# The recurrent gates of a two-layer hybrid trunk: from split operands to plain fp32 in 64x64 tiles

## The chip, the cores and the metric
One core of one Trainium2 chip. The time is the device time of one execution of the whole program in microseconds; lower is better. Three runs of the kernel before gave 2337.05, 2337.07 and 2337.18 us; the median, 2337.07, is the time before.

## The reference
Two layers over 1024 positions of 2048 features in fp32. Each layer makes six parts from one projection of the normalized input, runs two mixers on them, gates both, and projects back. The change concerns `r` and `i` of the second mixer alone: 16 diagonal blocks of 64x64 weights each, applied to the convolved input.

```
h = rmsnorm(x, norm_gain[l])
q, k, v, g_attn, x_rnn, g_rnn = split(h @ w_in[l])
attn = swa_sink_attention(q, k, v, sinks)        # window of two chunks of 64
xc = causal_conv(x_rnn, conv_w, conv_b)          # width 4
xb = xc.reshape(b, s, 16, 64)
r = sigmoid(einsum('bshi,hij->bshj', xb, w_r) + b_r)
i = sigmoid(einsum('bshi,hij->bshj', xb, w_i) + b_i)
log_a = -8 * r * softplus(-lru_param)
u = sqrt(-expm1(2 * log_a)) * (i * xc)
rnn = associative_scan(a = exp(log_a), u)
x = x + concat(attn * silu(g_attn), rnn * silu(g_rnn)) @ w_out[l]
```

After the second layer a last rmsnorm closes the trunk.

## The kernel before
**Tiling.** Features lie on the 128 partitions, positions in the free dimension. The sequence is worked in two halves of 512 positions (`h`), each through both layers (`l`). The projections are the bulk: per layer 25 groups (17 in, 8 out) of two 128-feature tiles over 16 tiles of input. They run as units. A unit is one slot `s` of 200 per layer; it takes a 128x512 piece of weights (two input tiles by 256 output features) and issues 12 matmuls of 128x512 (line 420).

**Splitting.** These matmuls have fp32r operands. To keep fp32 accuracy each operand is split in two parts: ScalarE copies it to fp32r (the high part), VectorE subtracts that from the original (the low part), and three products are added up: high by high, high by low, low by high. For weights that is `weight_hi` (line 636) and `weight_lo` (line 995), four buffers in a ring, three units ahead of TensorE.

**Order.** Each engine has a hand-written loop over `h`, `l`, `s`; at given slots other work is put behind or ahead of the unit. On TensorE these are scores (line 504), transposes of the probabilities (line 522) and values (line 534) at slots 36, 44, ... (`VISIT`), and the recurrent gates at `R0[j] + 5` and `R0[j] + 7`. `R0` is the slot at which the projection of recurrent tile `j` is complete: 48, 56, 64, 72, 88, 96, 104, 112.

**A recurrent tile** holds two blocks of 64 features, so its gates need four products with 64x64 weights: two blocks times `r` and `i`. After the projection VectorE scales (`conv`, slot `R0`), then makes the four taps of the convolution into `xc` (`taps`, slots `R0 + 1` and `R0 + 2`). ScalarE copies the gate weights to fp32r (`gate_weights_hi`, line 785) and the two blocks of `xc` (`conv_hi`, line 793), VectorE subtracts (`gate_weights_lo`, line 1169, and `conv_lo`, line 1176). The two parts of one block lie above each other in `xcut`, 64 partitions the high part and 64 the low part, and the weights of that block stand twice below each other in `gw`. So one matmul over 128 rows gives weight part times both parts of the input, two matmuls (one per part of the weights) give one block's `r` and `i`. This is `gate(h, l, j, part)`, line 553, once for each block:

```
for a in range(2):
    last = pe.matmul(ps_g[:, :], gwcut[:, part, a, :], xcut[:, part, :], start=a == 0, stop=a == 1)
```

Both blocks write the same PSUM bank `ps_g`, the second once ScalarE has read the first (`gate_out`, lines 803 and 805, slots `R0 + 6` and `R0 + 8`: two tanh of 64x512 each). The recurrence follows on both engines in slots `R0 + 9` to `R0 + 13`. `ps_g` and its neighbour `ps_t` also take the transposes.

**Queues.** All large loads are issued by SyncE in the order of the slots: the projection weights (line 335), each waiting for the low part of the unit in hand, and at slot `R0[j] - 8` the gate weights of tile `j` (line 359) into one of two buffers.

**Plain fp32 calls.** Scores, values and transposes take fp32 operands unsplit. Scores are 16 calls per visit with 64 rows, 64 columns of weights and 128 of data, in all four quarters of the array (two row halves, two column halves), the row halves into two banks. Values are 4 calls with 128 rows, 64 columns of weights and 256 of data, in the two column halves.

Of the kernel before, what the change touches and what calls it, by code (L numbers as in the profile page):

```python
# [7 lines left out]
F32 = mybir.dt.float32  # L8
# [5 lines left out]
P = 128  # L14
# [5 lines left out]
HD = 64  # L20
# [87 lines left out]
def build(nc, xt, w, gates, par, fgain, cossin, ident, out):  # L108
    with ExitStack() as ctx:
# [26 lines left out]
        acc = sb("acc", [TOK])  # L136
        gw = sb("gw", [GRING, 2, P])
        gwcut = sb("gwcut", [2, 2, P], F32R)
        khist = sb("khist", [DEPTH, CH])
# [26 lines left out]
        ps_tok = ps_t[:, 0, 0:HT // P]  # L166
        ps_half = ps_g[:, 0:HT]
        ps_ss = ps_t[:, :, :].rearrange("p a b -> p (a b)")

# [21 lines left out]
        op_hi = sem("op_hi")  # L191
        gw_hi = sem("gw_hi")
        xc_hi = sem("xc_hi")
        sq_done = sem("sq_done")
# [18 lines left out]
        op_lo = sem("op_lo")  # L213
        gw_lo = sem("gw_lo")
        xc_lo = sem("xc_lo")
        acc_done = sem("acc_done")
# [94 lines left out]
        def _(sp_):  # L311
# [16 lines left out]
            for h in range(HALVES):  # L328
                for l in range(DEPTH):
                    for s in range(SLOTS):  # L330
                        u = h * UNITS + l * SLOTS + s

                        sp_.wait_ge(w_lo, u + 1)
                        ahead = (u + RING if u + RING < TOTAL else u + RING - UPG) % UNITS
                        sp_.dma_start(wraw[:, u % RING, :],
                                      w[ahead // SLOTS, ahead % SLOTS]).then_inc(w_in[u % RING], 16)
                        if u + 3 < KT // 2:
                            x_load(0, u + 3)
                        if l == 0 and s in (4, TAB_LD):

                            sp_.wait_ge(q_done, per_layer(h, s // TAB_LD, AT, 1))
                            sp_.dma_start(tab[:, 0, :], cossin[0, h]).then_inc(tab_in, 16)
                            sp_.dma_start(tab[:, 1, :], cossin[1, h]).then_inc(tab_in, 16)
                        if l == 0 and s == 60:

                            if h > 0:
                                sp_.wait_ge(out_done_s, 16 * len(STORES_W) * h)
                            sp_.dma_start(x[:, :, :], xt[h]).then_inc(xres_in, 16)
                        for a, b in STORES_W:
                            if h > 0 and l == 0 and s == NS + 2 * b:  # L350

                                sp_.wait_ge(scaled, (h - 1) * KT + b)
                                sp_.dma_start(out[h - 1, :, a:b, :], x[:, a:b, :]).then_inc(out_done_s, 16)
                        if s + 8 in R0:
                            j = R0.index(s + 8)
                            n = l * RT + j

                            sp_.wait_ge(gw_lo, h * (DEPTH * RT) + (n + 1))
                            sp_.dma_start(gw[:, n % GRING, :, :], gates[l, j]).then_inc(gw_in[n % GRING], 16)
                        if l == 1 and s == O0 + 12 and h < LAST:  # L360

                            sp_.wait_ge(op_lo, at_op(h, 1, 1, KT - 1))
                            for i in range(KT // 2):
                                x_load(h + 1, i)
# [24 lines left out]
        def _(pe):  # L389
# [4 lines left out]
            pe.sem_inc(vt_done, 1)  # L394
            pe.sem_inc(g_done, 2 * GRING)

# [112 lines left out]
            def prob_transposes(h, l, p):  # L509
# [4 lines left out]
                else:  # L514
                    pe.wait_ge(vtok_done, per_layer(h, l, 2, 2))
                gates_read = sum(r + 7 < VISIT[p + 1] for r in R0)
                if gates_read:
# [19 lines left out]

            def gate(h, l, j, part):

                n = l * RT + j  # L540
                if part == 0:

                    pe.wait_ge(xc_lo, per_layer(h, l, 2 * RT, 2 * j + 2))
                    pe.wait_ge(gw_lo, h * (DEPTH * RT) + (n + 1 + GRING))
                    copied = sum(v < R0[j] + 5 for v in VISIT[1:NP + 1])
                    pe.wait_ge(pt_done, per_layer(h, l, NB, 2 * copied))
                    if j > 0:
                        pe.wait_ge(i_done, per_layer(h, l, 2 * RT, 2 * j))
                else:

                    pe.wait_ge(i_done, per_layer(h, l, 2 * RT, 2 * j + 1))
                for a in range(2):
                    last = pe.matmul(ps_g[:, :], gwcut[:, part, a, :], xcut[:, part, :], start=a == 0, stop=a == 1)  # L553
                last.then_inc(g_done, 1)

            for h in range(HALVES):
                for l in range(DEPTH):
                    for s in range(SLOTS):
# [20 lines left out]
                        for j in range(RT):  # L579
                            if s in (R0[j] + 5, R0[j] + 7):  # L580
                                gate(h, l, j, (s - R0[j] - 5) // 2)
            for i in range(UPG - 2):
# [43 lines left out]
        def _(act):  # L626
# [152 lines left out]

            def gate_weights_hi(h, l, j):  # L780
                n = l * RT + j

                act.wait_ge(gw_in[n % GRING], h * (16 * DEPTH * RT // GRING) + (16 * (n // GRING) + 16))
                act.wait_ge(g_done, h * (2 * DEPTH * RT) + (2 * n + 2 * GRING))
                act.activation(gwcut[:, :, 0, :], gw[:, n % GRING, :, :], ACT.Copy).then_inc(gw_hi, 1)

            def conv_hi(h, l, j):

                act.wait_ge(conv_done, per_layer(h, l, RT, j + 1))
                act.wait_ge(g_done, per_layer(h, l, 2 * RT, 2 * j) + 2 * GRING)  # L790
                for part in range(2):
                    rows = slice(HD * part, HD * part + HD)
                    act.activation(xcut[rows, part, :], xc[rows, :], ACT.Copy).then_inc(xc_hi, 1)  # L793

            def gate_out(h, l, j, part):

                act.wait_ge(g_done, per_layer(h, l, 2 * RT, 2 * j + part + 1) + 2 * GRING)
                if j > 0 and part == 0:
                    act.wait_ge(m2_done, per_layer(h, l, RT, j))
                if j > 1 and part == 0:  # L800
                    act.wait_ge(scan_done, per_layer(h, l, RT, j - 1))
                a, b = HD * part, HD * (1 - part)
                act.activation(r_in[a:a + HD, :], ps_g[a:a + HD, :], ACT.Tanh, scale=0.5,  # L803
                               bias=pars[a:a + HD, l, C_BR + j:C_BR + j + 1]).then_inc(r_done, 1)
                act.activation(i_in[j % 2][a:a + HD, :], ps_g[b:b + HD, :], ACT.Tanh, scale=0.5,
                               bias=pars[b:b + HD, l, C_BI + j:C_BI + j + 1]).then_inc(i_done, 1)
# [42 lines left out]
            for h in range(HALVES):  # L849
                for l in range(DEPTH):  # L850
                    for s in range(SLOTS):
# [58 lines left out]
                        if s == VT_TR + 1:  # L910
                            for i in range(2):
                                v_copy(h, l, i)
                        if s - 3 in R0:
                            conv_hi(h, l, R0.index(s - 3))
                        if s - 1 in G0:
# [5 lines left out]
                        for j in range(RT):  # L921
                            if s == R0[j] + 2:
                                gate_weights_hi(h, l, j)
                            if s == R0[j] + 10:
# [49 lines left out]
        def _(dve):  # L974
            dve.sem_inc(evac, 4)
            dve.sem_inc(q_done, 1)
            dve.sem_inc(gw_lo, GRING)
            dve.memset(eps[:, :], EPS).then_inc(dve_set, 1)
# [174 lines left out]

            def taps(h, l, j, part):
                for c in (0, 1) if part == 0 else range(2, CW):
                    wc = pars[:, l, C_CW + CW * j + c:C_CW + CW * j + c + 1]
# [6 lines left out]
                    else:  # L1163
                        dve.scalar_tensor_tensor(xc[:, :], src, wc, xc[:, :], ALU.mult, ALU.add).then_inc(conv_done, 1)

            def gate_weights_lo(h, l, j):
                n = l * RT + j
                dve.wait_ge(gw_hi, h * (DEPTH * RT) + (n + 1))
                dve.tensor_tensor(gwcut[:, :, 1, :], gw[:, n % GRING, :, :], gwcut[:, :, 0, :].bitcast(F32),
                                  ALU.subtract).then_inc(gw_lo, 1)  # L1170

            def conv_lo(h, l, j):
                for part in range(2):
                    a, b = HD * part, HD * (1 - part)
                    dve.wait_ge(xc_hi, per_layer(h, l, 2 * RT, 2 * j + part + 1))
                    dve.tensor_tensor(xcut[b:b + HD, part, :], xc[a:a + HD, :],  # L1176
                                      xcut[a:a + HD, part, :].bitcast(F32), ALU.subtract).then_inc(xc_lo, 1)

# [64 lines left out]
            for h in range(HALVES):  # L1243
                for l in range(DEPTH):
                    for s in range(SLOTS):
# [20 lines left out]
                        if s - 2 in R0:  # L1266
                            taps(h, l, R0.index(s - 2), 1)
                        if s - 4 in R0:
                            conv_lo(h, l, R0.index(s - 4))
                        if s - 3 in R0:  # L1270
                            gate_weights_lo(h, l, R0.index(s - 3))
                        for k in range(X_EARLY if h else RING, KT):
# [175 lines left out]
```

## Time and profile before

| | before |
|---|---|
| median of the runs, us | 2337.07 |
| span of the profiled execution, us | 2335.3 |
| TensorE busy, us | 2328.8 |
| VectorE busy, us | 1389.5 |
| ScalarE busy, us | 1257.0 |
| projection matmuls (line 420), busy us | 2176.9 |
| recurrent gate matmuls (line 553), busy us | 39.8 |
| copies of the convolution to its high part (line 793), busy us | 40.4 |
| subtractions for its low part (line 1176), busy us | 43.9 |

The page gives the profiled execution by its span, from the first to the last instruction; the device time of a run, about 1.8 us more, holds what lies around it. Busy times of one engine overlap for matmuls, which are pipelined: a matmul of 128x512 is on record for about 390 ns, and the next begins before it ends. The price of a group of matmuls is therefore read from starts, not from durations.

### The profile page before, as it was taken

To read this page: it belongs to the slowest core of one execution; us is meant where nothing else is said; L and a number is where in the kernel's file an instruction comes from. 1 tells how busy PE (TensorE), PEld (TensorE's weight loads), DVE (VectorE), ACT (ScalarE), POOL (GpSimd) and SP (SyncE) were. 2 spreads that over 40 slices of the span, in tenths; PEclk is the share of its full clock that TensorE was granted. 3 is DMA by queue.
4 is the path that set the end of the run, shared out by engine and by line. 5 is a ranking of instruction groups with operands and counts; after the bars stand their busy time and mean duration, and the time that the engine had idled before them with its cause. 6 is when DMAs were issued, how large, how long until landed. Compare 5 with 4: busy or idle time off the path is not lost.

```text
span 2335.3 us, 31126 instructions
## 1 busy us (share of the span) xinstructions
PE 2328.8 (100%) x11466; PEld 1916.2 (82%) x11466; DVE 1389.5 (60%) x2239; ACT 1257.0 (54%) x2379; POOL 0.8 (0%) x10
## 2 busy tenths in 40 slices
PE   9999999999999999999999999999999999999999
PEld 8888888888888888888888888888888888888888
DVE  7557667434546767744475676764354467676335
ACT  7457666324445767534464576652244557665333
POOL 0000000000000000000000000000000000000000
PEclk9999999999999999999999999999999999999999
DMA  5334323333332233353334432233333332323334
GB/s 192 102 108 144 93 89 94 100 95 100 95 98 86 84 93 88 95 171 92 99 113 137 171 108 88 88 100 95 98 96 95 93 93 84 89 91 96 99 95 140
DMA packets 127016, 244.42 MB, mean 105 GB/s; under 512 B 14352, under 2 KB 18704, under 8 KB 126096
## 3 DMA queue, kind: packets, MB, share of 16 engines
q1 hardware_dynamic: 126288, 242.28, 33.7%
q8 instruction: 90, 1.47, 0.3%
q14 instruction: 62, 0.51, 0.1%
q10 hardware_dynamic: 576, 0.16, 0.0%
HBM read 234.00 MB, written 8.39 MB: 104 GB/s over the span
## 4 chain that ended last, share of the span: by engine, by line
PE 100%; DVE 0%; issue 0%; POOL 0%; POOLq 0%
PE proj L420 93%; PE ps_sc L504 1%; PE proj L534 1%; PE ps_g L553 1%; PE proj L436 1%; PE ps_g L522 1%; PE ps_t L522 1%; PE proj L463 0%; PE ps_t L392 0%; PE ps_t L478 0%; PE proj L612 0%; PE ps_t L488 0%; PE ps_g L488 0%; PE ps_sc L612 0%; PE ps_t L592 0%; DVE mixed L1388 0%
## 5 line engine op out<-in xcount | busy, mean ns | idle before, releaser
L420 PE MATMUL proj<-operand,wcut 128*128 128x512 f32 x9480 | 2176.9, 390 | 0.0
L420 PEld LDWEIGHTS proj<-operand,wcut 128*128 128x128 f32 x9480 | 1776.7, 188 | 378.6 <-issue 7.0
L995 DVE TENSOR_TENSOR wcut<-wraw,wcut 128x512 fp32r<-128x512 f32 x804 | 555.0, 690 | 878.2 <-ACT wcut L636 874.8
L636 ACT ACTIVATE wcut<-wraw 128x512 fp32r<-128x512 f32 x803 | 506.3, 631 | 900.0 <-PE proj L420 882.6
L761 ACT ACTIVATE prob<-ps_sc,stat 128x128 f32<-128x128 f32 x256 | 89.7, 362 | 0.6
L719 ACT ACTIVATE gy<-proj 32x512 f32<-32x512 f32 x144 | 84.9, 589 | 3.8
L793 ACT ACTIVATE xcut<-xc 64x512 fp32r<-64x512 f32 x64 | 40.4, 631 | 44.6 <-issue 23.0
L676 ACT ACTIVATE sqr<-x 128x512 f32<-128x512 f32 x62 | 36.8, 635 | 45.9 <-DVE x L1207 45.7
L1024 DVE TENSOR_TENSOR acc<-acc,sqr 128x512 f32<-128x512 f32 x80 | 55.2, 691 | 4.9
L761 ACT ACTIVATION_READ_ACCUMULATOR prob<-ps_sc,stat 128x1 f32 x256 | 51.6, 202 | 0.0
L1162 DVE SCALAR_TENSOR_TENSOR xc<-xr,pars,xc 128x512 f32<-128x512 f32 x64 | 47.9, 749 | 1.4
L1006 DVE TENSOR_TENSOR operand<-mixed,operand 128x512 fp32r<-128x512 f32 x64 | 41.7, 688 | 10.3 <-ACT operand L658 9.6
L824 ACT ACT_TABLE_LOAD x32 | 41.1, 1283 | 11.7 <-DVE mu L1192 11.3
L1176 DVE TENSOR_TENSOR xcut<-xc,xcut 64x512 fp32r<-64x512 f32 x64 | 43.9, 686 | 2.1
L803 ACT ACTIVATE sqr<-ps_g,pars 64x512 f32<-64x512 f32 x64 | 43.7, 683 | 1.3
L1207 DVE TENSOR_TENSOR x<-proj,x 128x512 f32<-128x512 f32 x62 | 39.9, 685 | 2.2 <-PE proj L420 1.3
L749 ACT ACTIVATE gt<-gy 128x512 f32<-128x512 f32 x56 | 35.5, 633 | 8.3 <-DVE gy L1108 7.0
L1120 DVE TENSOR_TENSOR mixed<-mixed,gy 128x512 f32<-128x512 f32 x56 | 38.8, 692 | 1.9
L1144 DVE TENSOR_TENSOR prob<-prob,stat 128x1024 f32<-128x1024 f32 x32 | 39.2, 1225 | 1.1
L1130 DVE TENSOR_REDUCE stat<-ps_sc 128x8 f32<-128x1024 f32 x32 | 39.2, 1224 | 1.1
L553 PE MATMUL ps_g<-xcut,gwcut 128*128 128x512 f32 x128 | 39.8, 391 | 0.0
L1103 DVE TENSOR_TENSOR gy<-proj,rstd 128x512 f32<-128x512 f32 x56 | 38.6, 689 | 1.4
(161 smaller groups left out, 1200.4 us busy)
## 6 DMA issues: line engine op xcount, KB each, us to landing
wraw<-in_w SPq DMA_DIRECT2D x804, 256.0 KB, 2.6
x<-in_xt SPq DMA_DIRECT2D x2, 4096.0 KB, 12.8
mixed<-in_xt SPq DMA_DIRECT2D x14, 512.0 KB, 7.3
gw<-in_gates SPq DMA_DIRECT2D x32, 128.0 KB, 2.6
out<-x SPq DMA_DIRECT2D x4, 1024.0 KB, 4.9
out<-mixed SPq DMA_DIRECT2D x7, 512.0 KB, 2.6
tab<-in_cossin SPq DMA_DIRECT2D x8, 256.0 KB, 3.4
mixed<-in_xt SPq DMA_DIRECT2D x4, 256.0 KB, 3.7
```

The source lines that it names most:

```text
L420: last = pe.matmul(bank[:, :], wcut[:, u % RING, a, c:c + P], operand[:, k, b, :], start=(k == 0 and n == 0), stop=(k == KT - 1 and n == 2))
L522: last = pe.transpose(ps_tr[i][:, 2 * odd + pair, :], prob[:, odd, i, pair, :], idn[:, :])
L553: last = pe.matmul(ps_g[:, :], gwcut[:, part, a, :], xcut[:, part, :], start=a == 0, stop=a == 1)
L636: act.activation(wcut[:, u % RING, 0, :], wraw[:, u % RING, :], ACT.Copy).then_inc(w_hi, 1)
L719: act.activation(gy[dst:dst + 32, 1, :], bank_of(l, tile)[src:src + 32, :], ACT.Copy).then_inc(shift_done, 1)
L761: act.activation(prob[:, odd, i, pair, :], ps_s[:, odd, i, pair, :], ACT.Exp, scale=HD ** -0.5, bias=stat[:, 1, odd, i, pair:pair + 1], ac ...
L803: act.activation(r_in[a:a + HD, :], ps_g[a:a + HD, :], ACT.Tanh, scale=0.5, bias=pars[a:a + HD, l, C_BR + j:C_BR + j + 1]).then_inc(r_done, 1)
L995: dve.tensor_tensor(wcut[:, u % RING, 1, :], wraw[:, u % RING, :], wcut[:, u % RING, 0, :].bitcast(F32), ALU.subtract).then_inc(w_lo, 1)
L1006: dve.tensor_tensor(operand[:, k, 1, :], mixed[:, k, :], operand[:, k, 0, :].bitcast(F32), ALU.subtract).then_inc(op_lo, 1)
L1024: ins = dve.tensor_tensor(acc[:, :], acc[:, :], sqr[:, k % 2, :], ALU.add)
L1162: mark(dve.scalar_tensor_tensor(xc[:, :], src, wc, xc[:, :], ALU.mult, ALU.add))
L1176: dve.tensor_tensor(xcut[b:b + HD, part, :], xc[a:a + HD, :], xcut[a:a + HD, part, :].bitcast(F32), ALU.subtract).then_inc(xc_lo, 1)
```

## The change
The gates are no longer split. `gw` holds the fp32 weights once: its upper 64 rows are block 0, `[w_r | w_i]`, its lower 64 rows block 1, `[w_i | w_r]`. `gate(h, l, j)` is one visit at slot `R0[j] + 5` and issues four fp32 calls of 64 rows, 64 columns of weights and 512 of data, one per block and gate: block 0 into bank `ps_t`, block 1 into `ps_g`, the two gates of a block into the two halves of the partitions. The first block's tanhs read `ps_t`, the second's `ps_g`, at the slots of before. The four split steps on ScalarE and VectorE go, with their semaphores. The gate load on SyncE is half as large and waits for TensorE's visit two tiles earlier; the first tap of a tile waits for the visit of the tile before, which reads `xc`.

```diff
-        gw = sb("gw", [GRING, 2, P])
-        gwcut = sb("gwcut", [2, 2, P], F32R)
+        gw = sb("gw", [GRING, P])
...
+        ps_gate = [ps_t[:, :, :].rearrange("p a b -> p (a b)"), ps_g]
...
-                            sp_.wait_ge(gw_lo, h * (DEPTH * RT) + (n + 1))
-                            sp_.dma_start(gw[:, n % GRING, :, :], gates[l, j]).then_inc(gw_in[n % GRING], 16)
+                            sp_.wait_ge(g_done, h * (DEPTH * RT) + (n + 1))
+                            sp_.dma_start(gw[:, n % GRING, :], gates[l, j]).then_inc(gw_in[n % GRING], 16)
...
-            pe.sem_inc(g_done, 2 * GRING)
+            pe.sem_inc(g_done, GRING)
...
-                gates_read = sum(r + 7 < VISIT[p + 1] for r in R0)
+                gates_read = sum(r + 5 < VISIT[p + 1] for r in R0)
...
-            def gate(h, l, j, part):
+            def gate(h, l, j):
 
                 n = l * RT + j
-                if part == 0:
-
-                    pe.wait_ge(xc_lo, per_layer(h, l, 2 * RT, 2 * j + 2))
-                    pe.wait_ge(gw_lo, h * (DEPTH * RT) + (n + 1 + GRING))
-                    copied = sum(v < R0[j] + 5 for v in VISIT[1:NP + 1])
-                    pe.wait_ge(pt_done, per_layer(h, l, NB, 2 * copied))
-                    if j > 0:
-                        pe.wait_ge(i_done, per_layer(h, l, 2 * RT, 2 * j))
-                else:
-
-                    pe.wait_ge(i_done, per_layer(h, l, 2 * RT, 2 * j + 1))
-                for a in range(2):
-                    last = pe.matmul(ps_g[:, :], gwcut[:, part, a, :], xcut[:, part, :], start=a == 0, stop=a == 1)
+                pe.wait_ge(conv_done, per_layer(h, l, RT, j + 1))
+                pe.wait_ge(gw_in[n % GRING], h * (16 * DEPTH * RT // GRING) + (16 * (n // GRING) + 16))
+                copied = sum(v < R0[j] + 5 for v in VISIT[1:NP + 1])
+                pe.wait_ge(pt_done, per_layer(h, l, NB, 2 * copied))
+                if j > 0:
+                    pe.wait_ge(i_done, per_layer(h, l, 2 * RT, 2 * j))
+                for col in range(2):
+                    for blk in range(2):
+                        rows = slice(HD * blk, HD * blk + HD)
+                        last = pe.matmul(ps_gate[blk][HD * col:HD * col + HD, :], gw[rows, n % GRING, HD * col:HD * col + HD],
+                                         xc[rows, :], start=True, stop=True)
                 last.then_inc(g_done, 1)
...
-            def gate_weights_hi(h, l, j):
...
-            def conv_hi(h, l, j):
...
-                act.activation(r_in[a:a + HD, :], ps_g[a:a + HD, :], ACT.Tanh, scale=0.5,
+                act.activation(r_in[a:a + HD, :], ps_gate[part][a:a + HD, :], ACT.Tanh, scale=0.5,
...
-                act.activation(i_in[j % 2][a:a + HD, :], ps_g[b:b + HD, :], ACT.Tanh, scale=0.5,
+                act.activation(i_in[j % 2][a:a + HD, :], ps_gate[part][b:b + HD, :], ACT.Tanh, scale=0.5,
...
             def taps(h, l, j, part):
+                if part == 0:
+                    dve.wait_ge(g_done, per_layer(h, l, RT, j) + GRING)
...
-            def gate_weights_lo(h, l, j):
...
-            def conv_lo(h, l, j):
...
-    gates = np.tile(np.stack([first, second], axis=3), (1, 1, 2, 1, 1))
+    gates = np.concatenate([first, second], axis=2)
```

How TensorE's list runs from one pass of scores to the next transposes, before (`proj` is a bank of the projections, `ps_sc` the scores, `ps_t` and `ps_g` the two shared banks; line 420 is the projection, line 553 the gates, line 522 the transposes):

```order
L504 MATMUL ps_sc<-kboth,q 64x128 x16
L420 MATMUL proj<-operand,wcut 128x512 x12
L553 MATMUL ps_g<-xcut,gwcut 128x512 x2
L420 MATMUL proj<-operand,wcut 128x512 x24
L553 MATMUL ps_g<-xcut,gwcut 128x512 x2
L420 MATMUL proj<-operand,wcut 128x512 x60
L522 MATMUL ps_t<-idn,prob 128x128 x4
```

The same place with the change (lines 500, 416, 546 and 518 are scores, projection, gates and transposes there):

```order
L500 MATMUL ps_sc<-kboth,q 64x128 x16
L416 MATMUL proj<-operand,wcut 128x512 x12
L546 MATMUL ps_t<-xc,gw 64x512
L546 MATMUL ps_g<-xc,gw 64x512
L546 MATMUL ps_t<-xc,gw 64x512
L546 MATMUL ps_g<-xc,gw 64x512
L416 MATMUL proj<-operand,wcut 128x512 x84
L518 MATMUL ps_t<-idn,prob 128x128 x4
```

The second visit is gone, and the 24 and 60 projections around it are one run of 84; the first visit holds four calls in two banks.

SyncE's queue around the gate weights' loads in the first layer, before (`w_lo` is the split of a unit's weights, `gw_lo` that of the gate weights):

```order
L335 DMA wraw<-in_w 128x512 [waits w_lo] x2
L359 DMA gw<-in_gates 128x256 [waits gw_lo]
L335 DMA wraw<-in_w 128x512 [waits w_lo] x8
L359 DMA gw<-in_gates 128x256 [waits gw_lo]
L335 DMA wraw<-in_w 128x512 [waits w_lo] x4
```

And with the change (`g_done` counts the visits on TensorE):

```order
L331 DMA wraw<-in_w 128x512 [waits w_lo] x2
L355 DMA gw<-in_gates 128x128 [waits g_done]
L331 DMA wraw<-in_w 128x512 [waits w_lo] x8
L355 DMA gw<-in_gates 128x128 [waits g_done]
L331 DMA wraw<-in_w 128x512 [waits w_lo] x4
```

The places are the same; size and semaphore differ.

## Rows read from the trace of the kernel before

**Rows 1.** The page's head: span, busy time by engine, chain that ended last.
```profile
span 2335.3 us, 31126 instructions
...
PE 2328.8 (100%) x11466; PEld 1916.2 (82%) x11466; DVE 1389.5 (60%) x2239; ACT 1257.0 (54%) x2379; POOL 0.8 (0%) x10
...
PE 100%; DVE 0%; issue 0%; POOL 0%; POOLq 0%
```

**Rows 2.** Waits: waiting engine and line, what it waited for, us, times, longest.
```profile
ACT wcut L636 <- PE proj L420: 882.6, 515, 3.4
```

**Rows 3.** Chain that ended last, two pieces: start us, us, what, count.
```profile
11.11 29.93 PE proj L420 x132
...
2105.64 195.88 PE proj L420 x864
```

**Rows 4.** Windows around these pieces: length, busy by engine, clock (last but two).
```profile
10.90:40.00 29.10, 29.10 (x130) 24.09 (x130) 27.25 (x42) 25.81 (x43) 0.00 (x0) 1.00 0.65 229
2106.00:2300.00 194.00, 194.00 (x857) 160.72 (x856) 90.27 (x136) 77.60 (x125) 0.00 (x0) 1.00 0.33 97
```

**Rows 5.** TensorE's groups by form: count, busy us, mean ns, idle before.
```profile
L553 PE MATMUL ps_g<-xcut,gwcut 128*128 128x512 f32 x128 | 39.8, 391 | 0.0
L504 PE MATMUL ps_sc<-kboth,q 64*64 64x128 f32 x1024 | 35.3, 276 | 0.0
L534 PE MATMUL proj<-probT,vtok 128*64 128x256 f32 x256 | 34.7, 392 | 0.0
```

**Rows 6.** Timeline of TensorE, scores to transposes with gates: start us, us, what.
```profile
157.51 3.03 PE L420 MATMUL proj<-operand,wcut 128*128 128x512 f32 x12
160.38 0.62 PE L553 MATMUL ps_g<-xcut,gwcut 128*128 128x512 f32 x2
160.84 5.65 PE L420 MATMUL proj<-operand,wcut 128*128 128x512 f32 x24
...
180.43 0.60 PE L522 MATMUL ps_t<-idn,prob 128*128 128x128 f32 x4
```

**Rows 7.** The same, scores to transposes without gates.
```profile
107.64 1.10 PE L504 MATMUL ps_sc<-kboth,q 64*64 64x128 f32 x32
108.67 22.10 PE L420 MATMUL proj<-operand,wcut 128*128 128x512 f32 x96
130.61 0.60 PE L522 MATMUL ps_t<-idn,prob 128*128 128x128 f32 x4
```

**Rows 8.** The same, values between two pairs of gates, then no values.
```profile
320.29 13.80 PE L420 MATMUL proj<-operand,wcut 128*128 128x512 f32 x60
334.02 1.08 PE L534 MATMUL proj<-probT,vtok 128*64 128x256 f32 x8
335.04 3.06 PE L420 MATMUL proj<-operand,wcut 128*128 128x512 f32 x12
337.94 0.62 PE L553 MATMUL ps_g<-xcut,gwcut 128*128 128x512 f32 x2
...
344.34 16.53 PE L420 MATMUL proj<-operand,wcut 128*128 128x512 f32 x72
360.71 0.62 PE L553 MATMUL ps_g<-xcut,gwcut 128*128 128x512 f32 x2
```

**Rows 9.** Narrow windows in scores and values: start of the first, time until the last ends.
```profile
107.64 0.34 PE L504 MATMUL ps_sc<-kboth,q 64*64 64x128 f32 x4
107.64 0.45 PE L504 MATMUL ps_sc<-kboth,q 64*64 64x128 f32 x8
...
334.02 0.44 PE L534 MATMUL proj<-probT,vtok 128*64 128x256 f32 x2
334.02 0.65 PE L534 MATMUL proj<-probT,vtok 128*64 128x256 f32 x4
```

**Rows 10.** Timeline of SyncE's queue, one gate load and the next projection load.
```profile
156.53 0.43 SPq L359 DMA_DIRECT2D gw<-in_gates  x1
162.09 0.33 SPq L335 DMA_DIRECT2D wraw<-in_w  x1
```

More of the change, by code:

```diff
@@ L191, in build @@
         op_hi = sem("op_hi")
-        gw_hi = sem("gw_hi")
-        xc_hi = sem("xc_hi")
         sq_done = sem("sq_done")
@@ L213, in build @@
         op_lo = sem("op_lo")
-        gw_lo = sem("gw_lo")
-        xc_lo = sem("xc_lo")
         acc_done = sem("acc_done")
@@ L579, in _ @@
                         for j in range(RT):
-                            if s in (R0[j] + 5, R0[j] + 7):
-                                gate(h, l, j, (s - R0[j] - 5) // 2)
+                            if s == R0[j] + 5:
+                                gate(h, l, j)
             for i in range(UPG - 2):
@@ L778, in attn_out @@
                 act.activation(to, value_bank(l, p), ACT.Copy).then_inc(attn_done, 1)
-            def gate_weights_hi(h, l, j):
[L781 to L785, printed above, removed]
-            def conv_hi(h, l, j):
[L789 to L793, printed above, removed]
             def gate_out(h, l, j, part):
-                act.wait_ge(g_done, per_layer(h, l, 2 * RT, 2 * j + part + 1) + 2 * GRING)
+                act.wait_ge(g_done, per_layer(h, l, RT, j + 1) + GRING)
                 if j > 0 and part == 0:
@@ L912, in _ @@
                                 v_copy(h, l, i)
-                        if s - 3 in R0:
-                            conv_hi(h, l, R0.index(s - 3))
                         if s - 1 in G0:
@@ L921, in _ @@
                         for j in range(RT):
-                            if s == R0[j] + 2:
-                                gate_weights_hi(h, l, j)
                             if s == R0[j] + 10:
@@ L976, in _ @@
             dve.sem_inc(q_done, 1)
-            dve.sem_inc(gw_lo, GRING)
             dve.memset(eps[:, :], EPS).then_inc(dve_set, 1)
@@ L1164, in taps @@
                         dve.scalar_tensor_tensor(xc[:, :], src, wc, xc[:, :], ALU.mult, ALU.add).then_inc(conv_done, 1)
-            def gate_weights_lo(h, l, j):
[L1167 to L1170, printed above, removed]
-            def conv_lo(h, l, j):
[L1173 to L1177, printed above, removed]
             def lru_z(h, l, j):
@@ L1267, in _ @@
                             taps(h, l, R0.index(s - 2), 1)
[L1268 to L1271, printed above, removed]
                         for k in range(X_EARLY if h else RING, KT):
```

## The prediction
> **What bounds the kernel now.** I read the page's head first: TensorE is busy for 2328.8 of 2335.3 us, and the chain that ended last is TensorE to 100% [rows 1]. Then the waits: ScalarE stood 882.6 us in 515 waits of its weight splitting, each of them for TensorE to free a buffer [rows 2]. So the time is the sum of what TensorE issues, and an instruction taken off ScalarE or VectorE is worth nothing by itself. The profiled execution has a span of 2335.3 us; the median of the runs is 2337.07, 1.8 us more for what lies around the span. I make the sum against the span and add the 1.8 back. About 0.2% (4.7 us) is what a measurement of this kernel can tell from no change.
>
> **The unit of account.** Every price below is a detour: what the projection stream loses when something else stands in it. The stream runs at one matmul in 0.2267 us: 195.88 us for 864, 29.93 us for 132 [rows 3], with the granted clock at 1.00, the 2.4 GHz level [rows 4].
>
> **What the change removes on TensorE.** Two visits per tile, 32 tiles (2 halves, 2 layers, 8), each of two 128x512 matmuls; the profile has the 128 of them [rows 5]. Between a pass of scores and the next transposes stand 96 projections. Where the gates of one tile lie among them, they take 180.43 - 157.51 = 22.92 us [rows 6]; where none do, 130.61 - 108.67 = 21.94 [rows 7]. The gates of a tile thus cost 0.98 us. A second way: a pair takes 160.84 - 160.38 = 0.46 from its start to the next projection [rows 6], and the 72 projections between two pairs take 360.71 - 344.34 = 16.37 [rows 8], 0.05 more than 72 x 0.2267 = 16.32. Twice 0.51 is 1.02. I take 1.01 (the second way is free of what scores leave behind), or 32.3 us in all.
>
> **What it adds on TensorE.** One visit per tile: four fp32 calls of 64x64 with 512 columns, on four distinct quarters of the array. No row of before shows this form. The two nearest are scores (16 fp32 calls in 64x64, 128 columns, all four quarters) and values (4 fp32 calls of 128x64, 256 columns, two column halves). Three things are to be seen in them.
> First, an fp32 call becomes two MATMUL records: 1024 for 32 visits x 16 calls, 256 for 32 x 4 [rows 5].
> Second, calls on different quarters run side by side, in steps. Of scores, the first four records are over after 0.34 us and the first eight after 0.45: a step of 0.11 for four records. Of values it is two records at a time, over after 0.44 and 0.65: a step of 0.21 to 0.22 [rows 9]. The step doubles with the columns (128 to 256) and does not grow with the number of quarters that share it; with 512 columns I extend it to 0.43.
> Third, all three then have the same length of steps: scores 32/4 = 8 of 0.11, values 8/2 = 4 of 0.215, the new gates 8/4 = 2 of 0.43, each 0.86 to 0.87.
> What is left is entering and leaving another tiling. One visit of values stands alone in the stream, between two gate pairs: 72 projections and the values take 337.94 - 320.29 = 17.65 us, against 16.37 for 72 projections between the same neighbours [rows 8]. It costs 1.28 us, so 0.42 above its steps. From its start to the next projection a visit of values takes 335.04 - 334.02 = 1.02 [rows 8], one of scores 108.67 - 107.64 = 1.03 [rows 7], so four quarters enter and leave about as two halves do.
> The gates have two steps where values have four. Since 2 x 0.11 exceeds 0.215 by 0.005, a step saved is worth next to nothing; I take 1.27. Bounds: above, 1.31, the 1.28 of values, the 0.01 that scores take more, and 0.02 for four differences of rows rounded to 0.01. Below, 1.21: the 1.02 of values hold four steps of 0.215 and 0.16 of start and end; how this divides the rows don't tell, and I let a smaller share of it, 0.06, vanish under a step of 0.43.
>
> **The sum.** 32 x (1.27 - 1.01) = +8.3 us; with 1.21 - 1.02 it is +6.1, with 1.31 - 0.98 it is +10.6. Span 2335.3 + 8.3 = 2343.6, time 2337.1 + 8.3 = **2345.4 us**.
>
> **What it takes off the others, priced at nothing.** ScalarE loses, per tile, two 64x512 copies and the copy of the gate weights, VectorE the three subtractions that go with them. The cover is TensorE's own stream, for which both wait [rows 2]. The four tanh evacuations of a tile stay in their slots.
>
> **What moves or waits.** (a) The visit stays where part 0 was, 12 projections after scores, so it shares no entry with them; the visit 24 later is gone. (b) TensorE waits for the convolution itself, not for its split: by the lists VectorE ends it three units (of 12 projections) ahead, the split was one unit ahead. (c) The gates now also write the bank of the transposes; the next transposes come 84 projections (19 us) later, and the tanhs that free it stand within three units (8 us). (d) VectorE's first tap of the next tile waits for the visit of this one; behind it stand the weight splits, but the tap comes four units after the visit. (e) On SyncE's queue the gate weights' load waited for a split that was long done; it now waits for TensorE's visit two tiles earlier. Where these lie 16 units apart (half of them) this bites: the load went at 156.53 [rows 10], and the visit it would wait for starts at 160.38 [rows 6] and ends near 161.6. Behind it stands the next projection load, which went at 162.09 anyway [rows 10]; the gate load takes 0.43, so the other is late by 0.1 us at most, and the ring holds four units of weights (10.9 us). Price 0. If that cover were gone, each half-microsecond late would be paid 16 times, 8 us.
>
> **Rivals.**
> *The column halves run in series* (slower still). Then the visit has four steps, not two: 0.86 us more, and 32 x 0.86 + 8.3 = +35.8, 2372.9 us. It decides if a quarter cannot take its weights while its neighbour in the same rows streams. For it: here the issue goes over the row halves first, in scores over the column halves. Against it: in scores two pairs share their rows, and still four records are over together [rows 9]. The Trainium skill, "TensorE: Matmul & The Clock Gate", Packing small matmuls, says that a weight load overlaps with running matmuls only if its row group differs. By that rule this rival would be the forecast; the scores rows speak against it.
> *Entering and leaving cost nothing* (not slower). Then a visit is 0.86, and 32 x (0.86 - 1.01) = -4.8: 2332.3 us, at the edge of what can be told. It decides if weights and data that are ready long before let the array change its tiling while the last projection drains; with 0.15 of the 0.42 left it is no change. Against it: the operands of values are ready units before their turn too, and the 0.42 are paid [rows 8]. The same section of the Trainium skill models a packed group as one matmul and 4 ns per further tile, with no price for the ends; by it this rival would be the forecast, and the trace disagrees with it by the 0.42.
> *The relief of the other engines shortens the stream* (faster). 9480 projections would have to gain 0.9 ns each to cancel 8.3 us and 1.4 ns to come out 4.7 us ahead, at 2332.4. Against it: with VectorE busy 27.25 and ScalarE 25.81 of 29.10 us [rows 4] the step is 29.93/132 = 0.2267; with 90.27 and 77.60 of 194.00 it is 195.88/864 = 0.2267 [rows 3].
>
> **How the numbers follow.** Forecast 0.88, its own range 2343.2 to 2347.7 (+6.1 to +10.6). Columns in series 0.06, ends free or nearly so 0.04, relief 0.02. Slower by over 0.2%: 0.88 + 0.06 = 0.94. Within 0.2%: 0.04 of the second rival, less 0.01 for its edge, 0.03. Faster: 0.02 + 0.01 = 0.03. With 0.88 inside its bounds the forecast alone holds the 8 in 10, and the range is its own.
>
> **What would show it.** Gate MATMUL records: 256 instead of 128, in two groups of four per visit, the second about 0.43 after the first. From the visit's start to the next projection about 1.0 us. The 96 projections with a gate visit take about 23.2 us, not 22.92. TensorE busy for the whole span, the stream's step still 0.2267, ScalarE and VectorE less busy without effect. It is wrong if there are four groups (then near 2373), if the visit takes under 0.9 us (then the ends are cheaper), or if the projections begin to wait for split weights (then SyncE's new wait counts).

## The result, and the profile after

The changed kernel takes 2346.05 us, median of four runs (2345.93 to 2346.47); the kernel before, four runs beside them, 2337.12 (2337.05 to 2337.38). The ratio is 1.0039, with a 95% interval of 1.0024 to 1.0053: slower by 8.9 us. The forecast was 2345.4, with a range of 2343.2 to 2347.7.

| | before | after |
|---|---|---|
| median, us | 2337.12 | 2346.05 |
| span of the profiled execution, us | 2335.3 | 2344.2 |
| VectorE busy, us | 1389.5 | 1336.3 |
| ScalarE busy, us | 1257.0 | 1205.4 |
| gate records on TensorE | 128 | 256 |

The page's head of the changed kernel, as [rows 1]:

```profile
span 2344.2 us, 31157 instructions
...
PE 2337.3 (100%) x11594; PEld 1895.8 (81%) x11594; DVE 1336.3 (57%) x2143; ACT 1205.4 (51%) x2283; POOL 0.8 (0%) x10
```

TensorE still fills the span. VectorE and ScalarE have 53 and 52 us less to do, and the time went up. Its timeline from one pass of scores to the next transposes, as [rows 6]:

```profile
157.79 3.02 PE L416 MATMUL proj<-operand,wcut 128*128 128x512 f32 x12
160.74 0.64 PE L546 MATMUL ps_t<-xc,gw 64*64 64x512 f32 x1
160.74 0.64 PE L546 MATMUL ps_g<-xc,gw 64*64 64x512 f32 x1
160.75 0.64 PE L546 MATMUL ps_t<-xc,gw 64*64 64x512 f32 x1
160.75 0.64 PE L546 MATMUL ps_g<-xc,gw 64*64 64x512 f32 x1
161.22 0.59 PE L546 MATMUL ps_t<-xc,gw 64*64 64x512 f32 x1
...
161.75 19.36 PE L416 MATMUL proj<-operand,wcut 128*128 128x512 f32 x84
180.95 0.60 PE L518 MATMUL ps_t<-idn,prob 128*128 128x128 f32 x4
```

Four records start within 0.01 us, the next four 0.48 later, and the stream goes on 161.75 - 160.74 = 1.01 after the start. The 96 projections with a gate visit take 180.95 - 157.79 = 23.16 us, against 22.92 in [rows 6]. The same price without scores beside it, as [rows 8]:

```profile
340.06 0.64 PE L546 MATMUL ps_t<-xc,gw 64*64 64x512 f32 x1
...
341.08 22.07 PE L416 MATMUL proj<-operand,wcut 128*128 128x512 f32 x96
363.08 0.64 PE L546 MATMUL ps_t<-xc,gw 64*64 64x512 f32 x1
```

96 projections between two visits take 22.00, which is 0.24 more than 96 x 0.2267 = 21.76. With 1.02 for the visit itself the detour costs 1.26 us. The same reading of the kernel before gave 2 x 0.51 = 1.02. So both readings, 23.16 against 22.92 and 1.26 against 1.02, put 0.24 us more on each tile.

One place was not in the sum: the sixth tile of a layer, whose visit follows the last transposes.

```profile
310.63 0.60 PE L518 MATMUL ps_t<-idn,prob 128*128 128x128 f32 x4
...
312.61 3.03 PE L416 MATMUL proj<-operand,wcut 128*128 128x512 f32 x12
313.23 0.64 ACT L803 ACTIVATE mu<-mu 128x512 f32<-128x512 f32 x1
...
314.91 0.59 ACT L764 ACTIVATE probT<-ps_g 128x512 f32<-128x512 f32 x1
...
315.73 0.13 PEld L546 LDWEIGHTS ps_t<-xc,gw 64*64 64x64 f32 x1 [0.51 <-issue]
315.76 0.61 PE L546 MATMUL ps_t<-xc,gw 64*64 64x512 f32 x1
```

Here 12 projections and the entry take 315.76 - 312.61 = 3.15 us instead of 160.74 - 157.79 = 2.95. ScalarE ended its copy out of `ps_g` at 315.50, and the gate's first weight load came 0.23 later. This happens once in each of the four layer passes. In the kernel before the same copy was in time:

```profile
309.05 0.60 PE L522 MATMUL ps_t<-idn,prob 128*128 128x128 f32 x4
...
312.83 0.59 ACT L770 ACTIVATE probT<-ps_g 128x512 f32<-128x512 f32 x1
...
313.88 0.62 PE L553 MATMUL ps_g<-xcut,gwcut 128*128 128x512 f32 x2
```

It ended at 313.42, 4.37 after the transposes began and 0.46 before the gates. Now it ends 315.50 - 310.63 = 4.87 after them.

One more piece of the difference between the two profiled executions is older than the first gate. In the chain that ended last, the piece that began at 11.11 and took 29.93 us [rows 3] reads now:

```profile
11.19 30.12 PE proj L416 x132
```

It ends at 41.31 instead of 41.04, 0.27 us late, before any line of the change has run; in the profiles of the experiments below the first matmul of this line starts anywhere from 10.8 to 11.6 us (10.9 before, 11.1 here), and none of them changes what comes ahead of it.

### The profile page after: what moved, and what is told of

Its sections match the earlier page's. It is cut to its first block, busy times and chain, and to the rows that moved or that the text cites. A ratio compares the mean times of both kernels' runs of the same rounds, so it can differ in the third digit from the quotient of the medians.

```text
span 2344.2 us, 31157 instructions
## 1 busy us (share of the span) xinstructions
PE 2337.3 (100%) x11594; PEld 1895.8 (81%) x11594; DVE 1336.3 (57%) x2143; ACT 1205.4 (51%) x2283; POOL 0.8 (0%) x10
## 4 chain that ended last, share of the span: by engine, by line
PE 100%; DMA 0%; DVE 0%; issue 0%; SPq 0%; DVEq 0%
PE proj L416 92%; PE ps_sc L500 1%; PE proj L530 1%; PE ps_t L546 1%; PE proj L432 1%; PE ps_t L518 1%; PE ps_g L518 1%; PE proj L459 0%; DMA wraw<-in_w 0%; PE ps_t L474 0%; PE ps_g L484 0%; PE proj L606 0%; PE ps_t L484 0%; PE ps_sc L606 0%; PE ps_t L586 0%; PE ps_g L546 0%
## 5 line engine op out<-in xcount | busy, mean ns | idle before, releaser
L1082 DVE SCALAR_TENSOR_TENSOR gy<-gt,gy 128x512 f32<-128x512 f32 x56 | 38.5, 687 | 1.0
L652 ACT ACTIVATE operand<-mixed 128x512 fp32r<-128x512 f32 x64 | 37.2, 622 | 0.8
L500 PEld LDWEIGHTS ps_sc<-kboth,q 64*64 64x64 f32 x1024 | 27.6, 133 | 11.3 <-issue 11.3
L500 PE MATMUL ps_sc<-kboth,q 64*64 64x128 f32 x1024 | 35.3, 276 | 0.0
```

Of the source, the lines that this page charges most:

```text
L500: last = pe.matmul(ps_s[HD * m:HD * m + HD, odd, i, pair, :], q[rows, TPK * kv + 2 * pair + m, CH * c:CH * c + CH], kboth[rows, kv, CH * c ...
```

## Experiments

There are eight kernels, the first four on one chip and the last four on another, each time with runs of the kernel before between them: 2337.00 us beside the first four, 2336.95 beside the last four.

**Are the ends a fixed price per visit, or does each group of calls pay them?**

```diff
-                for col in range(2):
+                for col in (0, 1, 0, 1):
                     for blk in range(2):
```

> The four calls of each gate visit are issued twice in a row (the second time over the same results). Theory: a visit is a fixed price for entering and leaving the 64x64 tiling, 0.42 us, and 0.43 us for each step of four records side by side. Then two steps more add 0.86 us per visit, 32 x 0.86 = 27.5 us: 2346.1 + 27.5 = 2373.6 us, and the trace shows a visit start to next projection of 1.88 us instead of 1.02. Rival: the 0.42 us belong to each group of four calls (a drain per group): 32 x 1.27 = 40.6 us more, 2386.7. Rival: calls that return to a quarter in use run in series, over 2400.

Measured: 2372.75 us, 26.7 above the changed kernel. Timeline of TensorE in one visit:

```profile
160.69 0.64 PE L546 MATMUL ps_t<-xc,gw 64*64 64x512 f32 x1
...
161.17 0.59 PE L546 MATMUL ps_t<-xc,gw 64*64 64x512 f32 x1
...
161.60 0.59 PE L546 MATMUL ps_t<-xc,gw 64*64 64x512 f32 x1
...
162.03 0.59 PE L546 MATMUL ps_t<-xc,gw 64*64 64x512 f32 x1
...
162.57 19.34 PE L416 MATMUL proj<-operand,wcut 128*128 128x512 f32 x84
```

Each row stands for the first of four. The steps are 0.48, 0.43, 0.43, then 0.54 to the stream: 1.88 in all, 0.86 more than with two steps. So a step costs 0.43 us and the ends are paid once per visit. By the medians the two steps cost 26.7 / 32 = 0.83 us, a little less than the 0.86 of the rows; where the missing 0.8 us of the whole is gained was not traced. The first step is 0.05 longer than the others, as it is in the trace of before (0.16 against 0.11 us in scores, 0.27 against 0.215 in values). So it does not vanish under a longer step; the lower bound of the forecast, which let 0.06 vanish, did not come true.

**Do the ends belong to the cut in rows or in columns?**

```diff
-                for col in range(2):
-                    for blk in range(2):
-                        rows = slice(HD * blk, HD * blk + HD)
-                        last = pe.matmul(ps_gate[blk][HD * col:HD * col + HD, :], gw[rows, n % GRING, HD * col:HD * col + HD],
-                                         xc[rows, :], start=True, stop=True)
+                for blk in range(2):
+                    rows = slice(HD * blk, HD * blk + HD)
+                    last = pe.matmul(ps_gate[blk], gw[rows, n % GRING, :], xc[rows, :], start=True, stop=True)
```

> Two calls of 64 rows by 128 columns of weights per visit instead of four of 64x64: the array is cut in row halves only. Theory: the ends are paid for any change of tiling, and the two row halves run side by side: two steps of 0.43 us as before, so 2346 within 1 us. Rival: the ends belong to the column cut: up to 32 x 0.42 = 13 us less, 2333. Rival: row halves run in series: 4 steps, 27 us more, 2373.

Measured: 2346.87 us (2346.81 to 2347.15), 0.8 above the changed kernel.

```profile
160.41 0.69 PE L545 MATMUL ps_t<-xc,gw 64*128 64x512 f32 x1
160.42 0.69 PE L545 MATMUL ps_g<-xc,gw 64*128 64x512 f32 x1
160.95 0.59 PE L545 MATMUL ps_t<-xc,gw 64*128 64x512 f32 x1
160.95 0.59 PE L545 MATMUL ps_g<-xc,gw 64*128 64x512 f32 x1
161.47 19.36 PE L416 MATMUL proj<-operand,wcut 128*128 128x512 f32 x84
```

Two records side by side do what four did, and the visit takes 161.47 - 160.41 = 1.06: 0.04 more, all of it in the first step (0.54 against 0.48). With values (columns cut only) and scores (both) this makes three tilings with about the same ends. Calls of half the rows and all columns are no cheaper than the quarters.

**Do the ends come from the tiling, or from plain fp32?** The gates become two calls over the whole array, one per gate; their weights are block diagonal, the zeros are multiplied along.

```diff
-                for col in range(2):
-                    for blk in range(2):
...
+                for col in range(2):
+                    last = pe.matmul(ps_gate[col], gw[:, n % GRING, col, :], xc[:, :], start=True, stop=True)
```

> The two gates as two plain fp32 calls over the whole array, weights block diagonal with zeros (128x128), one call per gate and bank; no tiling. Theory: no change of tiling, so no entry, and on leaving only what fp32 transposes leave (0.09 us late first projection); 4 records in series of 0.43 us are 1.71, together about 1.82 us per visit against 1.28: 2346.1 + 32 x 0.54 = 2363 us. Rival: the ends come from plain fp32 and not from the tiling: 1.71 + 0.42 = 2.13, 2373 us.

Measured: 2362.42 us (2362.37 and 2362.47).

```profile
157.44 3.02 PE L416 MATMUL proj<-operand,wcut 128*128 128x512 f32 x12
160.29 1.02 PE L544 MATMUL ps_t<-xc,gw 128*128 128x512 f32 x2
161.16 1.02 PE L544 MATMUL ps_g<-xc,gw 128*128 128x512 f32 x2
161.61 19.65 PE L416 MATMUL proj<-operand,wcut 128*128 128x512 f32 x84
181.10 0.60 PE L518 MATMUL ps_t<-idn,prob 128*128 128x128 f32 x4
```

The entry is that of the stream, 160.29 - 157.44 = 2.85 for 12 projections instead of 2.95. Start to start would mislead here, because the record of the next projection begins at 161.61, beside the last fp32 record, and lasts long; the stretch counts. It takes 181.10 - 157.44 = 23.66, 1.72 more than without gates [rows 7], and four records in series are 4 x 0.43 = 1.72. The medians give slightly more: (2362.42 - 2346.05) / 32 = 0.51 above the 1.26 of the changed kernel, so 1.77. Plain fp32 in the tiling of the stream thus has ends of 0.05 us at most; the 0.4 us are the price of changing the tiling and changing back.

**Is the work taken off ScalarE and VectorE worth something?**

```diff
+            def conv_hi(h, l, j):
+
+                act.wait_ge(conv_done, per_layer(h, l, RT, j + 1))
+                act.wait_ge(xc_lo, per_layer(h, l, 2 * RT, 2 * j))
+                for part in range(2):
+                    rows = slice(HD * part, HD * part + HD)
+                    act.activation(xcut[rows, part, :], xc[rows, :], ACT.Copy).then_inc(xc_hi, 1)
...
+                act.activation(gwcut[:, 0, :, :], ones[:, :].unsqueeze(1).to_broadcast([P, 2, P]),
+                               ACT.Copy).then_inc(gw_hi, 1)
```

VectorE's subtractions come back in the same way; TensorE reads none of it. (The two steps on the gate weights work on a buffer of ones of the same size.)

> The changed kernel, with the removed copies and subtractions of ScalarE and VectorE done again on buffers that nothing reads, at their old slots. Theory: both engines are under TensorE's cover, so the time stays at 2346.1 within 0.3 us; the visit of the sixth tile of each layer, which came 0.19 us late, stays late or comes a little later. Rival: the relief was worth something, then it is slower by up to some us; or the relief itself made the sixth visit late by changing the order in time, then 0.75 us faster.

Measured: 2346.13 us (2346.02 to 2346.95), the time of the changed kernel. VectorE is busy for 1390.5 us again and ScalarE for 1255.9, and the copies are there, with no effect on the time:

```profile
L1175 DVE TENSOR_TENSOR xcut<-xc,xcut 64x512 fp32r<-64x512 f32 x64 | 43.9, 686 | 2.1
...
L791 ACT ACTIVATE xcut<-xc 64x512 fp32r<-64x512 f32 x64 | 40.4, 631 | 45.6 <-issue 32.7 <-DVE xc L1163 12.0
```

So the work removed was worth nothing. TensorE waited for split weights once in the whole run, for 0.3 us. The sixth visit is late here too (3.15 us from the first of the 12 projections to the gates), so the lateness does not come from the relief.

**What does the sixth visit wait for?** ScalarE's copy of the last transposes is moved ahead of a square root that waits for VectorE.

```diff
-                                if s == VISIT[p + 1] + 1:
+                                if s == VISIT[p + 1] + 1 and p < NP - 1:
                                     prob_copy(h, l, p, i)
...
+                        if s == VISIT[NP]:
+                            for i in range(2):
+                                prob_copy(h, l, NP - 1, i)
                         for j in range(RT):
                             if s == R0[j] + 12:
                                 rnn_mult(h, l, j)
```

> The changed kernel, with one thing moved: ScalarE copies the last pair of transposed probabilities of a layer (slot 100) before the square root of the fifth tile, not after it. In the changed kernel this copy ended at 315.50 us and the visit of the sixth tile began at 315.76, its entry 0.505 us long against 0.318 of the others, in each of the four layer passes. Theory: this visit waits for the copy; then all 32 entries are 0.318, and the time falls by 4 x 0.187 = 0.75 us, to 2345.3. Rival: it waits for something else (the convolution, the tanhs before, the gate weights' load): the entry stays at 0.505 and the time at 2346.05.

Measured: 2345.70 us (2345.02 to 2346.05), 0.35 below the changed kernel, and 0.35 below the swapped order of the last experiment, which ran beside it on the same chip. The entry in the expectation is counted from the start of the last projection ahead of the visit, where I count from the first of the 12: 0.318 there is 2.95 here. TensorE and ScalarE:

```profile
312.94 3.03 PE L416 MATMUL proj<-operand,wcut 128*128 128x512 f32 x12
315.90 0.64 PE L546 MATMUL ps_t<-xc,gw 64*64 64x512 f32 x1
```

```profile
313.14 0.60 ACT L764 ACTIVATE probT<-ps_t 128x512 f32<-128x512 f32 x1 [1.74 <-PE proj L530]
313.63 0.59 ACT L764 ACTIVATE probT<-ps_g 128x512 f32<-128x512 f32 x1
314.24 1.28 ACT L803 ACT_TABLE_LOAD   x1
315.54 0.63 ACT L803 ACTIVATE mu<-mu 128x512 f32<-128x512 f32 x1
```

The entry is back at 315.90 - 312.94 = 2.96, in all four passes, so the wait was for the copy. The time fell by half of the 0.75 us that four such waits make. The trace shows the whole of it: from the start of the first projection to that of the last it is 2309.9 - 11.5 = 2298.4 us, and in the changed kernel 2310.3 - 11.1 = 2299.2. This kernel's profiled run began its long stream 0.4 us later, which is of the size of the missing half; whether that explains the medians too is open.

**The other half of the change alone: one visit, two banks, operands still split.** The edit is made to the kernel before; the first block's tanhs read `ps_t`, as in the changed kernel.

```diff
-                for a in range(2):
-                    last = pe.matmul(ps_g[:, :], gwcut[:, part, a, :], xcut[:, part, :], start=a == 0, stop=a == 1)
+                for part in range(2):
+                    for a in range(2):
+                        last = pe.matmul(ps_gate[part], gwcut[:, part, a, :], xcut[:, part, :], start=a == 0, stop=a == 1)
```

> The kernel before, split operands kept, with the other part of the change alone: both blocks in one visit per tile, four fp32r matmuls in a row into two banks. Theory: a pair costs 0.475 + 0.031 above the stream and four in a row 0.928 + 0.031, so a tile saves 0.047 us, 1.5 us in all; the visit of the sixth tile is late by about 0.19 x 4 = 0.75 us as in the changed kernel, because the second visit of the fifth tile no longer holds TensorE back. Together 2337.1 - 0.8 = 2336.3 us. Rival: no late sixth visit, 2335.6; rival: the lateness came with plain fp32 or the tiling, same number; the entry tells them apart (0.235 or 0.42).

Measured: 2336.19 us (2335.87 to 2336.58), against 2336.95 for before: 0.8 faster, as expected, though the interval of the ratio, 0.9987 to 1.0005, includes no change. The late entry is here too, and larger:

```profile
310.85 3.01 PE L421 MATMUL proj<-operand,wcut 128*128 128x512 f32 x12
314.01 0.70 PE L550 MATMUL ps_t<-xcut,gwcut 128*128 128x512 f32 x2
```

That is 3.16 us from the first of the 12 projections to the gates, 0.30 more than the 2.86 of the next kernel. It needs neither fp32 nor tiling: it comes when the second visit, which stood in TensorE's list between the fifth tile and the last transposes, is gone. TensorE reaches this place half a microsecond earlier, while ScalarE's copy stands where VectorE's work has put it. The size fits: here the gates start 0.26 after the copy has ended, in the kernel before they had 0.46, so there were 0.20 us to spare; of the 0.51 of the visit that went, 0.31 is left. With 64x64 tiles an entry takes 0.08 or 0.09 more anyway, and the lateness is 0.2. In all the kernels with one visit and the copy at its old place the sixth visit begins 5.11 to 5.15 us after the start of the last transposes.

**The same with the earlier copy.** Both edits above, on the kernel before.

> The same as the one-visit kernel with split operands, plus the earlier copy. Theory: all entries 0.235, 1.5 us less than before: 2335.6 us, the fastest of all. Rival: the late entry stays, 2336.3.

Measured: 2334.89 us (2334.38 to 2335.22, 11 runs) against 2336.95 (2336.62 to 2337.47, 23 runs): 2.06 us faster, ratio 0.9991 with an interval of 0.9982 to 1.0000. It is the fastest of all, and no run of it is as slow as the fastest of before. Timeline, as [rows 6], and the sixth tile:

```profile
158.15 3.03 PE L421 MATMUL proj<-operand,wcut 128*128 128x512 f32 x12
161.02 0.62 PE L550 MATMUL ps_t<-xcut,gwcut 128*128 128x512 f32 x2
161.48 0.63 PE L550 MATMUL ps_g<-xcut,gwcut 128*128 128x512 f32 x2
161.94 19.21 PE L421 MATMUL proj<-operand,wcut 128*128 128x512 f32 x84
180.99 0.60 PE L523 MATMUL ps_t<-idn,prob 128*128 128x128 f32 x4
...
311.30 3.02 PE L421 MATMUL proj<-operand,wcut 128*128 128x512 f32 x12
314.16 0.62 PE L550 MATMUL ps_t<-xcut,gwcut 128*128 128x512 f32 x2
```

Four gate matmuls in a row take 161.94 - 161.02 = 0.92, and the stretch 180.99 - 158.15 = 22.84, 0.08 less than with two visits: 32 times, 2.6 us, read from rows of 0.01. From the start of the first projection to that of the last it is 2299.4 - 11.6 = 2287.8 us, against 2301.1 - 10.9 = 2290.2 before: 2.4 less. The medians show 2.06, and here too the profiled run began its long stream late. The two kernels with the earlier copy begin it later (11.5 and 11.6) than all the others (10.8 to 11.2); whether that belongs to them or to the one execution profiled of each is not shown. I had counted 0.047 per tile, because I took the slow steps after a visit (0.03 us spread over the next ten) as paid once per visit; they are hardly there after the longer visit.

**Does the order of the four calls matter?**

```diff
-                for col in range(2):
-                    for blk in range(2):
+                for blk in range(2):
+                    for col in range(2):
```

> The changed kernel with the four calls issued over the column halves first and the row halves second, as scores do. Theory: four quarters start together whatever the order, visit start to next projection stays 1.02 us, time 2346.05 within 0.3. Rival: with two calls of the same rows behind each other the second's weights load only after the first's matmul: 4 steps, 1.88 us, 2373.

Measured: 2346.05 us (2345.65 to 2346.78), no difference. The quarters start together in either order.

## Why the prediction was right, point by point

*The bound.* Right: TensorE is the span before and after, and 54 and 51 us of work put back on VectorE and ScalarE changed nothing.

*What is removed: 1.01 us per tile.* Right, and so is what comes in its place: 1.26 by the same reading (forecast 1.27). The forecast took 0.26 between the two, the rows give 0.24, or 7.7 us for 32 tiles. The stream as a whole says what is right: the kernel with the early copy, which has the new detours and no late visit, takes 2298.4 us from the first projection to the last, the kernel before 2290.2. That is 8.2 us, against the 8.3 of the sum. That the two agree to 0.1 is partly luck, since 32 times a row of 0.01 is 0.3.

*Steps of 0.43 and quarters side by side.* Right, and shown by the visit that was doubled. The rival in which column halves run in series did not occur in either order. The Trainium skill's rule that it rested on, in "TensorE: Matmul & The Clock Gate", Packing small matmuls, that a weight load overlaps with running matmuls only if its row group differs, does not hold for the gates here: records of the same rows start within 0.01 us of each other, and their second weights are loaded at 160.79 to 160.81, while the first four records run. (The same section names a second case, a load into the array's background weight buffer, which would allow this; the trace doesn't show the buffer.)

*Ends of 0.42.* Right in size (1.26 - 0.86 = 0.40), and shown to be the change of tiling: with no change of tiling the same fp32 work takes its four steps, 1.72 us, and 0.05 more at most.

*The queue of SyncE, priced 0.* Right. The new wait is there, 58.0 us in 16 waits, half of the 32 loads:

```profile
SPq L355 <- PE ps_g L546: 58.0, 16, 5.0
```

The first such load went at 161.88, and the projection load behind it at 162.35, when VectorE had just ended the split it waits for (161.63 + 0.69 = 162.32).

```profile
161.63 0.69 DVE L969 TENSOR_TENSOR wcut<-wraw,wcut 128x512 fp32r<-128x512 f32 x1 [5.16 <-ACT wcut L630]
...
161.88 0.33 SPq L355 DMA_DIRECT2D gw<-in_gates  x1
...
162.35 0.34 SPq L331 DMA_DIRECT2D wraw<-in_w  x1
```

*What the sum lacked.* Under "what moves or waits" I priced the shared bank for what comes after the gates (the next transposes) and not for what comes before them. The visit already waited for the copies of the last transposes before the change; I took that wait as unchanged because its text is. But the visit of the fifth tile's second block no longer held TensorE back ahead of it, and this cost 0.19 us four times, about 0.75. With the 0.27 us from before the first gate, 8.2 + 0.75 + 0.27 = 9.2, and the last projection does start 2310.3 - 2301.1 = 9.2 us later. What follows it is some 0.3 us shorter in this profile, which leaves the 8.9 between the two spans. The forecast missed the median by 0.6; the late visits are the term that it lacked, while the 0.27 and the 0.3 lie outside the stretch that the change touches and are of the size by which executions differ. By its medians the early copy gave back only 0.35.

## What to carry to other kernels

Work off an engine that is not the bound buys nothing, so ask what the change adds on the one that is. Here four matmuls that filled the whole array with split operands (1.01 us in two visits, about 0.08 less in one) gave way to a form that needs no splitting but 0.86 us of steps and 0.4 us for changing the tiling and back. A tiled form pays its ends once per visit, so many steps should share one. Whether the ends go when the visit stands beside other work of the same tiling was not tried. And when a visit is taken out of a full engine's list, look at the next wait whose text has not changed: its slack was partly that visit.

## What the runs showed of the hardware

A plain fp32 call of 512 columns is two steps of 0.43 us, whether a step holds one record (whole array), two (row halves) or four (quarters). Changing the tiling costs about 0.4 us for going and coming back, with the first step 0.05 us longer than the rest when the calls have 64 columns of weights (0.48 against 0.43) and 0.11 longer when they have 128 and the rows are cut (0.54). Plain fp32 over the whole array has ends of 0.05 us at most. The small delays after a visit, 0.03 us in all over ten matmuls, were there after two fp32r matmuls and not after four; why is open.
